# Column-wise norms of a transposed activation: root and reciprocal on 128 columns instead of 512

## The reference

```python
def rms_norm_2(x, w):
    xf = x.astype(F32)
    y = xf * lax.rsqrt(jnp.mean(xf * xf, axis=-1, keepdims=True) + EPS)
    return (y * w.astype(F32)).astype(x.dtype)
```

## Time and profile before

| | |
|---|---|
| three runs | 3872.81, 3875.44 and 3876.08 us, median 3875.44 |
| the profiled execution | 3872.84 us, of which the span of the profile 3871.1 us |
| TensorE matmul | 3476.0 us busy, 90% of the span |
| TensorE weight load | 1605.3 us, 41% |
| VectorE | 1248.7 us, 32% |
| ScalarE | 649.1 us, 17% |
| mean granted TensorE clock | 0.944 of full speed |
| DMA in the second expert layer (slices 36 to 39 of 40) | 419 to 420 GB/s |

### The profile page before, as it was taken

How to read it: one execution, slowest core, us unless ns; L and a number is a source line. 1 busy time by engine, 2 the same in 40 slices (tenths; PEclk the granted TensorE clock), 3 DMA queues, 4 the chain that set the end, 5 groups by cost and what they waited for, 6 DMA issues and landing times. The chain is left out here.

```text
span 3871.1 us, 33380 instructions
## 1 busy us (share of the span) xinstructions
PE 3476.0 (90%) x13546; PEld 1605.3 (41%) x13546; DVE 1248.7 (32%) x2297; ACT 649.1 (17%) x1380; POOL 0.2 (0%) x4
## 2 busy tenths in 40 slices
PE   7999788999889798999875999999989778599998
PEld 3444343444344343555653433333335544333332
DVE  1110752010283426653555112212233452311112
ACT  1000441000161201111112111111011341211111
POOL 0000000000000000000000000000000000000000
PEclk9999999999999899999967999999999789799999
DMA  3333102333301112002301577676751001399995
GB/s 142 130 146 158 44 1 75 121 140 130 130 1 44 71 75 93 25 22 95 118 22 45 204 285 277 264 276 262 304 225 44 22 1 47 121 420 420 420 419 238
DMA packets 86529, 588.05 MB, mean 152 GB/s; under 512 B 12441, under 2 KB 13372, under 8 KB 15973
## 3 DMA queue, kind: packets, MB, share of 16 engines
q1 hardware_dynamic: 78624, 572.56, 37.3%
q10 hardware_dynamic: 7748, 13.30, 1.0%
HBM read 583.73 MB, written 2.10 MB: 151 GB/s over the span
## 5 line engine op out<-in xcount | busy, mean ns | idle before, releaser
L453 PE MATMUL ps<-mem 128*128 128x512 f32 x1152 | 506.4, 599 | 17.2 <-DVE mem L570 17.2
L1672 PE MATMUL ps<-mem 128*64 128x512 f32 x2048 | 470.5, 603 | 1.3 <-ACT mem L1619 0.7
L453 PEld LDWEIGHTS ps<-mem 128*128 128x128 f32 x1152 | 219.5, 192 | 300.9 <-issue 297.8
L1024 PE MATMUL ps<-mem 128*128 128x512 f32 (+1 forms) x768 | 253.0, 492 | 7.7 <-ACT mem L879 7.7
L1672 PEld LDWEIGHTS ps<-mem 128*64 128x64 f32 x2048 | 137.9, 137 | 293.3 <-issue 289.8
L1641 DVE SCALAR_TENSOR_TENSOR mem<-ps,mem 128x512 f32<-128x512 f32 x128 | 96.1, 751 | 357.7 <-PE ps L1601 354.8
L1024 PEld LDWEIGHTS ps<-mem 128*128 128x128 f32 x768 | 147.5, 193 | 113.4 <-issue 102.0
L797 PE MATMUL ps<-mem 128*128 128x512 f32 x384 | 167.1, 592 | 0.0
L450 PE MATMUL ps<-mem 128*128 128x512 f32 x384 | 167.0, 594 | 0.0
L1291 PE MATMUL ps<-mem 128*128 128x512 f32 (+1 forms) x384 | 142.0, 532 | 7.3 <-POOLq L174 7.3
L514 ACT ACTIVATE mem<-ps 128x512 f32<-128x512 f32 x48 | 28.7, 597 | 687.7 <-PE ps L453 687.7
(11 more groups left out here) (290 smaller groups left out, 3958.4 us busy)
## 6 DMA issues: line engine op xcount, KB each, us to landing
mem<-in_moe_w SPq DMA_DIRECT2D x384, 1024.0 KB, 7.8
mem<-in_w_in SPq DMA_DIRECT2D x48, 1024.0 KB, 9.1
mem<-in_ada_w SPq DMA_DIRECT2D x48, 1024.0 KB, 6.7
mem<-in_hy_w_in SPq DMA_DIRECT2D x24, 1024.0 KB, 6.5
mem<-in_w_out SPq DMA_DIRECT2D x12, 1024.0 KB, 8.8
mem<-in_k_win_l SPq DMA_DIRECT2D x8, 1024.0 KB, 6.9
mem<-in_hy_w_out SPq DMA_DIRECT2D x8, 1024.0 KB, 6.5
mem<-in_sw_w_in SPq DMA_DIRECT2D x6, 1024.0 KB, 5.9
```

The source lines that it names most:

```text
L453: m = mm(ps[:, j % 4, :], Wc[s][:, k, t * P:(t + 1) * P], HTL[:, k, :], start=(k == 0), stop=(k == KD - 1))
L1024: m = mm(ps[:, j % 4, 0:L], Wc[s][:, k, (j % 4) * P:(j % 4 + 1) * P], H[:, k, :], start=(k == 0), stop=(k == KD - 1))
L1672: m = mm(ps[64 * x:64 * x + 64, pair, :], lat(k), w[x][:, k % 4, :], start=(k == 0), stop=(k == KD - 1))
```

## The change

The sums of squares are no longer spread over all partitions by the matmul that makes them. The 512 tokens are cut into four blocks of 128 columns. Block g is multiplied by 32 columns of ones and lands on partitions 32g to 32g+31 of the same 128 columns of one bank (`pe_sums`): four small matmuls in the place of one. With 256 tokens there are two blocks of 64 partitions. Root and reciprocal then run on 128x128 values (`act_root`, `dve_invert`). Then `pe_spread` brings row 32g, by a matmul with a single row of ones, to all 128 partitions of one bank per block, and the stt reads its factor from these banks in PSUM, in a view of 4 banks by 128 columns. In `act_norm` and in the output phase ScalarE runs a root on one column (`act_load_root`) ahead of the wait for the sums.

In the output phase the head sums move behind the first bank of round 0 and go into one bank for all four heads, so that one root covers them. Their spreads stand behind the third and the fourth bank of round 0, and bank 0, the fifth, waits until VectorE has finished all four heads.

```diff
@@ -377,26 +377,60 @@
+        def act_root(A, roots, sums, n):
+            act(roots, sums, ACT.Sqrt, bias=eps_col, scale=1.0 / n).then_inc(A.mark("rstd"), 1)
+
+        def act_load_root(A):
+            act(MISC[:, 4:5], MISC[:, 1:2], ACT.Sqrt).then_inc(A.mark(), 1)
+
         def act_norm(A, src, sq, rs, n, bank, turn):
             for k in range(0, KD, 2):
                 act(sq[:, k, :], src[:, k, :], ACT.Square).then_inc(A.mark("squares"), 1)
+            act_load_root(A)
             A.e.wait_ge(S["stat"], turn)
-            act(rs, ps[:, bank, 0:n], ACT.Sqrt, bias=eps_col, scale=1.0 / D).then_inc(A.mark("rstd"), 1)
+            act_root(A, rs[:, 0:P], ps[:, bank, 0:P], D)
         def dve_squares(A, src, sq):
             for k in range(1, KD, 2):
                 tt(sq[:, k, :], src[:, k, :], src[:, k, :], ALU.mult).then_inc(A.mark("squares_v"), 1)
-        def pe_norm(A, sq, n, bank, turn):
+        def pe_sums(bank, x, start, stop, at=0):
+
+            groups = x.shape[-1] // P
+            rows = P // groups
+            for g in range(groups):
+                m = mm(ps[rows * g:rows * g + rows, bank, at:at + P], ONES[:, 0:rows], x[:, g * P:(g + 1) * P],
+                       start=start, stop=stop)
+            return m
+
+        def pe_spread(A, rs, n, banks, at=0):
+
+            rows = P // (n // P)
+            for g, bank in enumerate(banks):
+                m = mm(ps[:, bank, at:at + P], ONES[rows * g:rows * g + 1, :], rs[rows * g:rows * g + 1, 0:P],
+                       start=True, stop=True)
+            m.then_inc(A.mark("spread"), 1)
+
+        def spread(banks, at=0):
+
+            return ps[:, banks[0]:banks[-1] + 1, at:at + P]
+
+        def blocks(x):
+
+            return x.rearrange("p (g t) -> p g t", t=P)
+
+        def pe_norm(A, sq, rs, n, bank, turn, banks=None):
             for k in range(KD):
                 A.e.wait_ge(S["squares_v" if k % 2 else "squares"], (turn - 1) * 4 + k // 2 + 1)
-                m = mm(ps[:, bank, 0:n], ONES, sq[:, k, :], start=(k == 0), stop=(k == KD - 1))
+                m = pe_sums(bank, sq[:, k, :], k == 0, k == KD - 1)
             m.then_inc(A.mark("stat"), 1)
-
-        def dve_recip(A, rs, turn):
+            if banks:
+                A.e.wait_ge(S["inverted"], turn)
+                pe_spread(A, rs, n, banks)
+
+        def dve_invert(A, rs, turn):
             A.e.wait_ge(S["rstd"], turn)
-            nc.vector.reciprocal(rs, rs).then_inc(A.mark(), 1)
-            A.e.wait_ge(*A.last)
+            nc.vector.reciprocal(rs[:, 0:P], rs[:, 0:P]).then_inc(A.mark("inverted"), 1)
         hm = Map(AR_)
@@ -434,8 +468,11 @@
             return {"q": QT, "k": KT, "g": GT, "v": VN}[w][:, kind * 4 + t, :]
+        NORM_BANKS = (3, 4, 5, 6)
+
         def pe_hyb_proj(A, st):
-            A.e.wait_ge(S["rstd"], 1)
+            A.e.wait_ge(S["inverted"], 1)
+            pe_spread(A, RS, T, NORM_BANKS)
             for j in range(len(HK)):
@@ -500,7 +537,7 @@
             e = A.e
-            act(RS, ps[:, 7, :], ACT.Sqrt, bias=eps_col, scale=1.0 / D).then_inc(A.mark("rstd"), 1)
+            act_root(A, RS[:, 0:P], ps[:, 7, 0:P], D)
             wff = a["w_ff"][bass.ds(l, 1)].rearrange("o p n -> (o p) n")
@@ -565,9 +602,10 @@
             nc.vector.tensor_copy(v(LV_, N_LV), LSV[:, bass.ds(l, 1), :].rearrange("p o n -> p (o n)")).then_inc(A.mark(), 1)
-            dve_recip(A, RS, 1)
+            dve_invert(A, RS, 1)
+            A.e.wait_ge(S["spread"], 1)
             for k in range(KD):
-                stt(HTL[:, k, :], XT[:, k, :], lv("g_pre", k), RS, ALU.mult, ALU.mult).then_inc(A.mark("h_ready"), 1)
+                stt(blocks(HTL[:, k, :]), blocks(XT[:, k, :]), lv("g_pre", k), spread(NORM_BANKS), ALU.mult, ALU.mult).then_inc(A.mark("h_ready"), 1)
             A.e.wait_ge(S["const_in"], 48)
@@ -782,22 +820,26 @@
         def pe_hyb_out(A, st):
-            for h in range(4):
-                A.e.wait_ge(S["squares"], h + 1)
-                mm(ps[:, h, :], ONES, SQS[:, h, :], start=True, stop=True).then_inc(A.mark("stat"), 1)
             for n, c in enumerate(OUT_ORDER):
                 s = st.get()
                 for b in ((4, 5, 6, 7, 0, 1, 2, 3) if n == 0 else range(KD)):
-                    if n == 0 and b < 4:
-                        A.e.wait_ge(S["rstd"], b + 1)
+                    if n == 0 and b == 0:
+                        A.e.wait_ge(S["h_ready"], 4)
                     for k in range(4):
-                        if b == 0 and n == 2:
-                            A.e.wait_ge(S["h_ready"], k + 1)
                         m = mm(ps[:, b, :], Wr[s][:, k, b * P:(b + 1) * P], GT[:, 4 * c + k, :],
                                start=(n == 0 and k == 0), stop=(n == 2 and k == 3))
                         if b == 0 and k == 0 and n:
                             m.then_inc(S["w_used"], 2)
+                    if n == 0 and b == 4:
+                        for h in range(4):
+                            A.e.wait_ge(S["squares"], h + 1)
+                            m = pe_sums(0, SQS[:, h, :], True, True, at=h * P)
+                        m.then_inc(A.mark("stat"), 1)
+                    if n == 0 and b in (6, 7):
+                        for h in (0, 1) if b == 6 else (2, 3):
+                            A.e.wait_ge(S["inverted"], h + 1)
+                            pe_spread(A, RSH[:, h, :], T, HEAD_BANKS, at=h * P)
                     if n == 2:
                         m.then_inc(A.mark("psum_full"), 1)
                         if b == KD - 1:
@@ -808,14 +850,19 @@
                     st.next()
             pe_post_stat(A, KD - 2)
             pe_post_stat(A, KD - 1)
+            A.e.wait_ge(S["inverted"], 5)
+            pe_spread(A, RS, T, POST_BANKS)
             pe_next_stat(A, 4 + KD)
             end_phase(A)
+
+        HEAD_BANKS = (0, 1, 2, 3)
+        POST_BANKS = (1, 2, 3, 4)
         def pe_post_stat(A, k):
             if k == 0:
                 A.e.wait_ge(S["a_ready"], 1)
             A.e.wait_ge(S["squares"], 4 + k + 1)
-            m = mm(ps[:, 0, :], ONES, SQY[:, k, :], start=(k == 0), stop=(k == KD - 1))
+            m = pe_sums(0, SQY[:, k, :], k == 0, k == KD - 1)
             if k == KD - 1:
                 m.then_inc(A.mark("stat"), 1)
@@ -823,25 +870,26 @@
                 A.e.wait_ge(S["squares"], first + k + 1)
-                m = mm(ps[:, 7, :], ONES, SQ[:, k, :], start=(k == 0), stop=(k == KD - 1))
+                m = pe_sums(7, SQ[:, k, :], k == 0, k == KD - 1)
             m.then_inc(A.mark(), 1)
         SQS = v(QT_ + 2048, 4, 512)
-        RSH = v(QT_ + 4096, 4, 512)
+        RSH = v(QT_ + 4096, 4, P)
         YS = v(HT_, KD, 512)
                 act(SQS[:, h, :], QT[:, h, :], ACT.Square).then_inc(A.mark("squares"), 1)
-            for h in range(4):
-                A.e.wait_ge(S["stat"], h + 1)
-                act(RSH[:, h, :], ps[:, h, :], ACT.Sqrt, bias=eps_col, scale=1.0 / P).then_inc(A.mark("rstd"), 1)
+            act_load_root(A)
+            A.e.wait_ge(S["stat"], 1)
+            act_root(A, RSH.rearrange("p h t -> p (h t)"), ps[:, 0, :], P)
             for b in range(KD):
                 act(SQY[:, b, :], ps[:, b, :], ACT.Square).then_inc(A.mark("squares"), 1)
-            A.e.wait_ge(S["stat"], 5)
-            act(RS, ps[:, 0, :], ACT.Sqrt, bias=eps_col, scale=1.0 / D).then_inc(A.mark("rstd"), 1)
+            act_load_root(A)
+            A.e.wait_ge(S["stat"], 2)
+            act_root(A, RS[:, 0:P], ps[:, 0, 0:P], D)
             for k in range(KD):
@@ -849,16 +897,21 @@
             for h in range(4):
-                dve_recip(A, RSH[:, h, :], h + 1)
-                stt(QT[:, h, :], QT[:, h, :], SMALL[:, 8:9], RSH[:, h, :], ALU.mult, ALU.mult).then_inc(A.mark(), 1)
+                dve_invert(A, RSH[:, h, :], 1)
+            A.e.wait_ge(S["spread"], 4)
+            for h in range(4):
+                q = blocks(QT[:, h, :])
+                stt(q, q, SMALL[:, 8:9], spread(HEAD_BANKS, h * P), ALU.mult, ALU.mult).then_inc(A.mark(), 1)
                 A.e.wait_ge(*A.last)
                 nc.vector.tensor_copy(YS[:, b, :], ps[:, b, :]).then_inc(A.mark("a_ready"), 1)
-            dve_recip(A, RS, 5)
+            dve_invert(A, RS, 2)
+            A.e.wait_ge(S["spread"], 5)
             for k in range(KD):
-                stt(YS[:, k, :], YS[:, k, :], lv("g_post", k), RS, ALU.mult, ALU.mult).then_inc(A.mark(), 1)
+                stt(blocks(YS[:, k, :]), blocks(YS[:, k, :]), lv("g_post", k), spread(POST_BANKS), ALU.mult, ALU.mult)\
+                    .then_inc(A.mark(), 1)
                 scaled = A.last
@@ -878,16 +931,18 @@
                 act(H[:, k, :], H[:, k, :], ACT.Identity, bias=mod(layer, which, k, n)).then_inc(A.mark("h_ready"), 1)
-        def dve_mod_norm(A, n, sq, rs, layer, which, norm, turn):
+        def dve_mod_norm(A, n, sq, rs, layer, which, norm, turn, banks):
             L, X, H = side(n)
```

(26 more changed lines are left out.)

11 lines of the change are left out of this document (6 added, 5 removed).

## The result

The changed kernel takes 3828.16 us (median of 4 runs, 3823.62 to 3829.11), the kernel before 3874.76 beside it: a ratio of 0.9878, 95% interval [0.9861, 0.9895]. In a second measurement, on the chip of the last experiments, it took 3823.22 against 3874.97: 0.9868 [0.9853, 0.9883]. The change takes 47 to 52 us away. The profiled execution of after is the fastest of the first four, 3823.62, with a span of 3821.8 against 3871.1: 49.3 less.

The account below looks back on a forecast made before the run. The prediction took TensorE to bound the kernel, so a norm costs only what it keeps TensorE from starting. Its terms sum to -46.2 us against the profiled 3872.84, giving 3826.6; it predicted 3828 us, range 3814 to 3846.

Parts of the forecast that it names:

- cold, 0.8: Sums of a norm: at a low clock, 0.8 us from a chunk's squares to its sum.
- Hyena term: Latent norm of the Hyena mixer: sums end 7.6 us earlier; with root, reciprocal and spread -9.5 us.
- The context norm: Hyena mixer's context side: table load and small root end later than the sums; -3.1 us in all.
- The attention's norm and the last norm: Windowed attention and end: latent rows repeat at -7.7 us each, attention's context norm adds tenths; -7.9 and -7.7 us.
- The post norm: Norm behind a layer, twice: cheaper steps of round 2, earlier last sum, shorter root and reciprocal; -6.6 us each.
- The heads: Output phase, twice: bank 0 waits for all four heads' scalings, then the clock falls; +6.4 us each.
- The first expert layer: Its norms and gate: gate logits begin 10.4 us earlier, 2.2 added for the clock; -8.2 us.
- The second expert layer: Its norm: all savings end in the gate logits' wait for the DMA of the router's weights; 0 us.
- Rival 1: Small matmuls are bound by their issue; chance 0.14.
- Rival 2: Reading the factor from PSUM slows the stt; at the bound +6 us, 3832 us; chance 0.07.
- Rival 3: Groups of 128 columns don't overlap, a pass costs 0.12 us; 62 us more, 3888 us; chance 0.08.
- rival 4: TensorE stays warm after the heads' wait and in the expert layer, spreads warm; -11 us, 3816 us; chance 0.10.

Follow-up runs that it names:

- experiment 2: Changed kernel with the sums of every norm but the heads' again as whole matmuls, roots reading diagonal blocks in pieces: 3880.32 us.
- experiment 1: Changed kernel with the output phase's heads done as before (whole sums, four roots and reciprocals on 512 columns, no spread): 3811.93 us.
- Experiment 7: Changed kernel with the context norms of Hyena mixer and first expert layer in four groups of 64 tokens, not two of 128: 3822.64 us.
- experiments 5 and 6: Second expert layer's router weights loaded ahead of the expert weights: in the changed kernel 3804.47 us, in the kernel before 3864.70 us.

## Why the prediction was right, and where it was not

Predicted 3828, measured 3828.16, and 3823.22 in the second measurement. That the first agrees to 0.2 us is luck: the profiled pair lies 49.3 apart and not 46.2, with 8.6 in a stretch that no term of the sum has, and several terms miss in opposite directions. What carries the prediction is that nearly every term has the right size.

- **The sums: right in kind, a little too large in one place.** The round of 0.109 us is 0.027 a pass, the price that the prediction used; by experiment 2 the sums are worth some 37 to 42 us (an estimate). What failed is "cold, 0.8" from the last square to the sum's end: that is the price of one chunk, and at clock 0.50 TensorE is not up to date when the last chunk comes. Eight chunks take 16 x 0.213 = 3.4 us, the squares 2.2. Sized so, the Hyena term is -8.2 and not -9.5, and the mark there shows -12.7 for -14.1. The context norm misses by the same reason: its sums take 3.4, at a clock of 0.53 to 0.59, and they, not the table load (it and the small root are over at 1777.9), are what the root waits for (it starts at 1778.98).
- **Root, reciprocal, spread: right** to 0.05 us each.
- **The attention's norm and the last norm: right.** From the last matmul of the experts to the first projection, and to the end of the span, both take 7.8 us less, 7.9 and 7.7 forecast. The rest of their rows in the table (-9.5 and -6.9) is the experts themselves, which the change doesn't touch.
- **The post norm: right**, -6.5 between the marks for -6.5. Its steps gained 0.31 each in pitch (4.30 to 3.99), not 0.43. What a change of tile shape costs was the author's estimate here and in the heads' block, where the traces show only the wholes: 1.08 us for 32 sum passes, of which eight rounds of 0.109 are 0.87, and 1.46 for both sets of spreads (1.4 forecast).
- **The heads: right in mechanism and size.** +6.0 and +5.8 by experiment 1, +6.4 forecast, with an idle stretch of 5.75. Two of its terms were off and partly cancel: bank 4 did not take over the 1.95 of cold passes, and the passes behind the wait lost 3.0, at a mean clock of 0.62, and not 2.0. At the 0.52 of their first 6 us a pass would take 0.83, an estimate from 0.431, where 0.86 was forecast. (The 3.1 beside the forecast's 2.0: the 16 passes of the earlier trace rows take 9.98 us, warm ones 6.9; the mean clock there was 0.71.)
- **The first expert layer: 0.9 more** than forecast, out of two misses. The gate logits began 9.1 us earlier and not 10.4, since the context's sums ended 2.8 behind their squares and not 0.8; and they stayed warm in spite of the idle time (10.49 us in both kernels, at clock 1.00), where 2.2 had been added. Experiment 7 shows the case that I had priced: started 2.0 us earlier, at a clock of 0.84, they lose 2.0.
- **The second expert layer: 0 was right in kind.** The DMA hid the norm, as experiments 5 and 6 show, but the stretch was not neutral: the router's load, measured from the last output matmul, came in 1.5 us later and the logits ran 0.9 slower behind the longer idle time (9.36 us at a clock of 0.75, 8.42 at 0.83). In all +2.5.
- **The attention: not foreseen.** I gave stretches without a change the same time. This one took between 232.7 and 242.4 us in thirteen profiles in which its code is the same, with the clock between 0.79 and 0.84. Without its 8.6 the profiled pair would show -40.7, inside the range and 6 short of the sum. How much of the 8.6 is in the medians no run shows: the profiled execution is the fastest of its four by 4 us.

Rival 1 (small matmuls bound by their issue, chance 0.14) is out: a pass in groups costs 0.027 us, and 64 of them take 2.21 in the first expert layer, at the pace of the squares (2.19); what the issue of one costs by itself no run shows. Rival 2 is out: eight stt take 5.36 us from PSUM, 5.39 before. Rival 3 is out, but its price was good: without overlap a pass costs 0.11 us (0.12 said), beyond the break-even of 0.10. The overlap is what this change lives on. Of rival 4 the gate logits stayed warm (clock 1.00), and of the spreads some were short: 0.50 us in the expert layers, where the clock was 1.00; the 0.81 in the Hyena mixer stand at 0.50, those in the first norm at 1.00. Behind the heads' wait TensorE ran at 0.62.

## What to carry to other kernels

A sum over partitions whose result has one row needs no more of TensorE's columns than its column groups: four blocks of tokens at once cost what one does (here a round of four 0.109 us, a pass alone 0.11), and what follows works on a quarter of the columns (root 0.37 us for 0.69, reciprocal 0.95 for 3.35). Count such passes in rounds at the clock that the place has (0.109 at 1.00, 0.213 at 0.50), and compare with what feeds them (eight squares in 2.2 us). When a new producer chain hangs on passes in TensorE's own queue, look for the earliest place at which their input is ready: moving the 32 one-row passes up, the last 16 by two banks, was worth as much as undoing the change there. A norm that ends in a wait for a DMA gains nothing until the DMA moves (the wait for the router's weights grew from 15.73 to 19.58 us); look what was issued in front of it. And look behind the norm too: in experiment 7 a saving of 1.5 us ended in the wait for the next matmul's weights.
